# GpSimd takes one operand split of the up projection in the first pair of the first two groups

## The reference

```python
x = layer_norm(DEEPNORM_ALPHA * x + heads @ w_out, ln_mix_g, ln_mix_b)
h = jnp.square(jax.nn.relu(x @ w_ff1))          # 1024 -> 4096, the up projection
x = layer_norm(DEEPNORM_ALPHA * x + h @ w_ff2, ln_ffn_g, ln_ffn_b)
```

## Time and profile before

| | us |
|---|---|
| median of three runs | 2411.53 |
| the profiled execution | 2409.59 |
| its span | 2407.9 |
| PE busy in the span | 2356.0 (98%) |
| DVE busy | 1569.4 (65%) |
| ACT busy | 1102.3 (46%) |
| POOL busy | 183.8 (8%) |

### The profile page before, as it was taken

How to read it: one execution, slowest core, us unless ns; L and a number is a source line. 1 busy time by engine, 2 the same in 40 slices (tenths; PEclk the granted TensorE clock), 3 DMA queues, 4 the chain that set the end, 5 groups by cost and what they waited for, 6 DMA issues and landing times. The chain is left out here.

```text
span 2407.9 us, 34854 instructions
## 1 busy us (share of the span) xinstructions
PE 2356.0 (98%) x12028; PEld 2058.7 (85%) x12028; DVE 1569.4 (65%) x2207; ACT 1102.3 (46%) x1820; POOL 183.8 (8%) x245
## 2 busy tenths in 40 slices
PE   7999989999999989999999999999999999999998
PEld 6888877999788889999999788888888888888887
DVE  8555366766666787786666655556566866764657
ACT  4111146887211265556556544445444444443333
POOL 2000001221223200000000000000000100000002
PEclk9999999999999999999999999999999999999999
DMA  8765776222466766677677655558877887787663
GB/s 303 281 265 229 273 212 225 77 68 88 127 229 245 282 243 245 262 267 269 239 264 266 258 205 196 211 198 309 279 225 212 271 299 226 211 277 257 194 195 118
DMA packets 220608, 547.85 MB, mean 228 GB/s; under 512 B 21704, under 2 KB 90952, under 8 KB 200908
## 3 DMA queue, kind: packets, MB, share of 16 engines
q1 hardware_dynamic: 204416, 488.19, 58.2%
q0 software_dynamic: 16080, 58.20, 7.6%
HBM read 365.95 MB, written 180.36 MB: 227 GB/s over the span
## 5 line engine op out<-in xcount | busy, mean ns | idle before, releaser
L71 PE MATMUL e_bank<-e_hi,e_lo 128*128 128x512 f32 x1120 | 435.8, 389 | 0.1
L72 PE MATMUL e_bank<-e_lo,e_hi 128*128 128x512 f32 x1120 | 435.7, 389 | 0.0
L73 PE MATMUL e_bank<-e_hi 128*128 128x512 f32 x1120 | 435.7, 389 | 0.0
L2362 DVE TENSOR_TENSOR e_lo<-e_raw,e_hi 128x896 fp32r<-128x896 f32 (+1 forms) x168 | 190.0, 1135 | 126.7 <-ACT e_hi L2317 126.5
L2317 ACT CAST e_hi<-e_raw 128x896 fp32r<-128x896 f32 (+1 forms) x168 | 165.2, 983 | 204.0 <-PE e_bank L73 198.1
L71 PEld LDWEIGHTS e_bank<-e_hi,e_lo 128*128 128x128 f32 x1120 | 210.2, 188 | 44.6 <-DVE e_lo L2362 1.0
L72 PEld LDWEIGHTS e_bank<-e_lo,e_hi 128*128 128x128 f32 x1120 | 210.2, 188 | 43.7
L73 PEld LDWEIGHTS e_bank<-e_hi 128*128 128x128 f32 x1120 | 210.2, 188 | 43.5
L71 PE MATMUL u_bank<-u_x_hi,u_wa_lo 128*128 128x384 f32 (+1 forms) x576 | 207.5, 360 | 4.1 <-ACT c_vt_raw L2060 3.9
L71 PE MATMUL u_bank<-u_x_hi,u_wb_lo 128*128 128x384 f32 (+1 forms) x576 | 203.5, 353 | 6.6 <-DVE u_x_first L1885 3.3
L73 PE MATMUL u_bank<-u_x_hi,u_wa_hi 128*128 128x384 f32 (+1 forms) x572 | 205.8, 360 | 0.0
(11 more groups left out here) (334 smaller groups left out, 4919.2 us busy)
## 6 DMA issues: line engine op xcount, KB each, us to landing
u_w_sum<-s_ws SPq DMA_DIRECT2D x33, 1024.0 KB, 4.8
c_vt_raw<-w_ff SPq DMA_DIRECT2D x24, 1024.0 KB, 7.0
c_q_raw<-w_ff SPq DMA_DIRECT2D x24, 1024.0 KB, 7.1
s_h<-c_k_raw SPq DMA_DIRECT2D x32, 768.0 KB, 6.9
e_raw<-s_t SPq DMA_DIRECT2D x96, 256.0 KB, 3.7
e_raw<-s_h SPq DMA_DIRECT2D x112, 192.0 KB, 2.8
ab_place<-w_ff SPq DMA_DIRECT2D x18, 1024.0 KB, 8.5
s_h<-c_k_raw SPq DMA_DIRECT2D x96, 192.0 KB, 2.6
```

The source lines that it names most:

```text
L71: tensor.matmul(out, w_lo, m_hi, start=first, stop=False, skip_group_check=again)
L72: tensor.matmul(out, w_hi, m_lo, start=False, stop=False, skip_group_check=again)
L73: return tensor.matmul(out, w_hi, m_hi, start=False, stop=last, skip_group_check=again)
L2362: dve.tensor_tensor(part(lo, n), part(raw, n), part(hi, n).bitcast(F32), ALU.subtract).then_inc(split, 1)
```

## The change

The low part of the seventh operand goes from DVE to POOL in the first pair of the first two groups (`g < LAST`); in the third group DVE keeps it. POOL makes it behind the loads of its group once all seven high parts are there, and raises a semaphore of its own. DVE only counts `x_split` on in its place. PE waits for the new semaphore too before P3 of these two pairs. In the first group DVE's `wa_low_raw` follows directly behind the count.

```diff
-        x_hi_done, x_split = al.sem("x_hi_done"), al.sem("x_split")
+        x_hi_done, x_split, x_last_split = al.sem("x_hi_done"), al.sem("x_split"), al.sem("x_last_split")
@@ gpsimd, in the loop over groups, behind the loads of x
+                if g < LAST:
+                    lo = x_slot(g, NPROD - 1, False)
+                    pool.wait_ge(x_hi_done, (g + 1) * NPROD)
+                    pool.tensor_tensor(lo.bitcast(F32R), lo, x_slot(g, NPROD - 1, True).bitcast(F32), ALU.subtract
+                                       ).then_inc(x_last_split, 1)
@@ vector, body
                 if start:
-                    x_low(g, 6)
+                    if g < LAST:
+                        dve.sem_inc(x_split, 1)
+                    else:
+                        x_low(g, 6)
                     if g == 0:
                         wa_low_raw(n + 1, 1 - s)
@@ tensor, body
                     pe.wait_ge(x_split, g * NPROD + j + 1)
+                    if start and g < LAST and j == NPROD - 1:
+                        pe.wait_ge(x_last_split, g + 1)
```

## The result

The change costs about 4 us: a median of 2416.2 us (21 runs, 2412.67 to 2420.25) against 2412.35 us before (21 runs), a difference of 3.9 us. The ratio of the two is given as 1.0018 with a 95% interval of 1.0012 to 1.0024, that is 4.3 us (2.9 to 5.8). One run of the kernel before took 4923.36 us, for which no trace shows a reason; the other 20 lie between 2409.55 and 2415.49, and without it the median is 2412.23. The forecast was +2.8 us, a change too small to count by its bound of 0.2%. That held, but the loss is clear of the scatter, and the time lies 0.2 us above the range given. The profiled execution took 2414.37 us, its span is 2412.7 us.

A forecast was written before the change was run, and what follows sets the result against it. PE, busy 98% of the span, was taken as the bound, so DVE matters only where PE waits. First group 0, second 1.2, clock fall 1.6 make +2.8 us on 2411.53: 2414.3 us, range 2411.2 to 2416.0.

The forecast's parts named there:

- nothing is won or lost, within 0.1 us: First group's first pair: POOL subtracts right behind the cast, P3 starts at 863.57 instead of 863.61; cost 0.
- Second group: Second group's first pair: POOL holds up DVE's h_sums by 2.9 us, delaying c22 and P3; 1.2 us lost.
- twice the cast's read: POOL's 1536-column subtraction: one-input cast scales to 1.56 us, two inputs one after the other make 3.1 us.
- The clock: Second group: PE idle 3.0 us before P3, then a granted-clock fall as after an earlier 2.47 us; +1.6 us.
- Rival 1: Second group: as forecast, but the clock holds; +1.2 us, 2412.7 us; chance 0.32.
- The sum: Whole kernel: first group 0, second group 1.2 and clock fall 1.6 make +2.8 us, 2414.3 us; chance 0.48.
- DVE keeping the pair (2): Second group: DVE goes on while work is in line, POOL enters only at 1099.40; +0.1, 2411.6 us; chance 0.07.
- no shut-out (3): Wide POOL subtraction doesn't shut DVE out; second group -1.8 us, first nothing; 2409.8 us; chance 0.07.
- 4.7 us for POOL (4): POOL's subtraction takes 4.7 us in both groups: 1.5 + 2.8 + 1.6 = +5.9, 2417.4 us; chance 0.06.
- The small parts: PE's added semaphore wait and DVE's count in place of an instruction: nothing, 0.1 us at most each.
- Lost stays lost: From 1120 to 1308 us PE has no gap, so time lost before stays lost and later loads and copies move along.

The follow-up runs named there:

- the early landing: The kernel after, profiled again unchanged; ACT waited 0.43 us for the first group's seventh-operand load; P7 to next P1 took 7.67 us, time 2414.69 us.
- the run with PE kept busy: Kernel after plus unread matmuls ahead of P3's waits, 7 in the first group and 16 in the second: 2414.66 us, ratio 1.0013.
- the two groups alone: Kernel after with POOL's subtraction in only one group: first group 2411.94 us, ratio 1.0004; second group 2415.75 us, ratio 1.0015.
- the unused subtraction: Kernel before plus an equally wide POOL subtraction nobody reads in the second group; DVE keeps its work, P3 waits for both: one time, 2416.68 us.
- the semaphores alone: Kernel after with all its semaphores and waits, but POOL only signals and DVE subtracts: 2412.84 us, ratio 1.0005.
- the kernel with the first group: Kernel after with POOL's subtraction in the first group only: 2411.94 us, ratio 1.0004; the two runs on the second chip took 2409.28 and 2412.04 us.
- a new order on VectorE: Kernel before; in the second group's first pair x_low(6) goes right behind x_low(5), and wa_low_raw behind c22: 2411.55 us, ratio 1.0002.

## Why the prediction was wrong, step by step

**The step that failed is that of the first group: "nothing is won or lost, within 0.1 us".** The working was right for the execution it was read from, as the early landing shows (7.67 against 7.64 us). What it took as given was that the cast ends where the earlier trace rows had it. There the cast ended at 860.32 and x_low(6) began only at 861.72, since it stands behind u3 and c22 on DVE: 1.4 us of slack, in which a late load disappears (after 2.09 us of wait for it, in the kernel before, the cast ended at 861.54 and x_low(6) began at 861.83). POOL starts right behind the cast. It takes 1.7 us longer and uses just that slack, so load, cast, POOL and P3 become one chain without any. A late load, which the kernel before also has, then costs 1.45 us at a full clock (the run with PE kept busy), and raises P3's idle time from 0.9 to 2.3 us or more, after which the clock fell all six times (3.47 to 3.72 us for P3's step, against 2.23): 1.2 to 1.5 us more. With 1.15 us of wait for the load the stretch was 7.96 us and the clock held. In the mean of the eight profiles with the full subtraction there and no extra matmuls the first stretch is 9.74 us, 2.1 over that of before. No run made the load late or early at will; what its lateness costs is read from executions in which it happened to be one or the other.

**Second group: right in mechanism, too small.** P3 is released by c22, DVE's first h_sums instruction is held up, and POOL goes first: all as forecast. (The cast that releases POOL is that of the seventh operand, j = 6; the prediction's "sixth" is a slip, and its time of 1095.73 is the right one.) The loss was 1.60 us instead of 1.2, since POOL took 3.46 us and not the 3.1 of twice the cast's read. The excess of 0.36 us makes 1.56. The estimate of 3.4 us from the Trainium skill (GPSIMD Engine Reference, section on elementwise side by side) was the better one; the trace agrees with it at 3.46.

**The clock: right in size, not certain.** A fall was counted in for the second group. It came in four of the five profiles with the full subtraction and an idle P3 there (3.30 or 3.33 us), where it cost 1.4 to 1.8 us, but not in the profile taken with the result. In all 20 profiles an idle time of 2.29 us or more before one of the two P3 was followed by a fall 12 times of 13, and one of 1.78 us or less never; the third group is less regular (last section). Rival 1 (the clock holds) is what the profile after shows in that place; as a forecast of the mean it would have been too low.

**The sum.** The second stretch has a mean of 15.43 us over those five profiles, +2.9 us; with the +2.1 of the first that makes +5.0, where the times say +4.3 (2.9 to 5.8). By the traces the second group's +2.9 is the forecast's whole +2.8, and what was missing is the first group. The times of the two groups alone, +1.0 (-1.2 to +3.1) and +3.6 (1.4 to 5.8), are too coarse to confirm this division, and by themselves don't show that the first group costs anything. Of the 1.9 us between the forecast of 2414.3 and the measured 2416.2, moreover, 0.8 is no effect of the change: the kernel before itself has 2412.35 in 21 runs, where three runs had given 2411.53.

**The rivals.** DVE keeping the pair (2) and no shut-out (3) are refuted by the held-up h_sums instruction, and by the unused subtraction; 4.7 us for POOL (4) by 3.46. None of them was about the load. The small parts at nothing hold: 7.60 and 12.47 us with the semaphores alone.

**Lost stays lost** holds only roughly. With the beginning of the up projection as the common start, and one execution of each kernel, the kernel after was 2.88 us late at the end of the first stretch, 1.79 before the second, 3.39 behind it and 3.0 at the end of the program.

## What to carry to other kernels

Before work goes to an engine that starts earlier but takes longer, ask what slack the old place had against its producer: a wait can be the same length in one trace and still have lost its tolerance for a late load. One profile doesn't show how a load's landing scatters, so take it from several, or count a microsecond or two of lateness in as a case. And where both inputs of a wide GpSimd instruction are in SBUF, look first whether a new order on VectorE does the same: here it took 1.1 us from the stretch (too little for the time to show), while the move put 1.6 on.

## What the hardware showed unexpectedly

- The same load, in the kernel before, was waited for 0.40 us in one execution and 2.09 in another, on two chips; on the second chip alone the kernel with the first group had 1.80 and 1.15 us, and on one chip the kernel after 0.43 and 1.96.
- An idle PE of 3.33 us once kept its clock of 1.00 (2.4 GHz) and once went to 0.54, that is mostly at 1.2 GHz, in two kernels that do the same there.
- At the start of the third group the clock scatters in kernels of every kind. The earlier trace rows has an idle time of 2.47 us before P2 and a fall; in 19 of the 20 profiles the idle time there was 2.04 to 3.08 us, and in 11 of these 19 the clock fell. Such a fall mostly costs nothing that lasts: from P2 to P3 it is 14.31 to 14.33 us in 17 profiles, since the next wait, some 1.5 us after most falls and 3.15 without one, takes up the difference (14.66 to 15.09 in the other three).
- The wait before P3 of the third group, 3.12 to 3.16 us in the nine profiles with no fall at P2, was followed by a fall in five of them, and this one lasts. With the semaphores alone, which otherwise behave as the kernel before, P3's step took 4.37 us against 2.82, and 220 matmuls behind P2's first it was still 1.6 us behind. So single executions differ by this much for a reason that the change has no part in. Its P3 and the next P1, and PE's clock of 0.58 between them:

```profile
1347.51 0.47 PE L71 MATMUL u_bank<-u_x_hi,u_wb_lo 128*128 128x512 f32 x1 [3.16 <-DVE u_x_first L1888]
1351.88 0.44 PE L71 MATMUL u_bank<-u_x_hi,u_wa_lo 128*128 128x512 f32 x1
...
1348.00:1351.50 3.50, 3.50 (x11) 2.70 (x11) 1.19 (x2) 1.26 (x2) 0.00 (x0) 0.58 0.03 11
```

- POOL's subtraction of a tile from itself took 2.93 us, of two different tiles 3.46.
